# Moving the tail of the group norm into the next pair of heads, in an RWKV-7 recurrence on TensorE

## The reference, cut to what matters

```python
kk = kk / jnp.maximum(jnp.sqrt(jnp.sum(kk * kk, axis=-1, keepdims=True)), 1e-12)   # the key norm
a_vec, b_vec = -kk, kk * a_h
S = S * w_t + (S @ av_t) (x) bv_t + v_t (x) k_t ;  y_t = S @ r_t                    # over the tokens
mu, var = mean(y), mean((y - mu)**2)                                               # over the 64 of a head
yn = (y - mu) * lax.rsqrt(var + GN_EPS) * lnx_w + lnx_b                            # the group norm
out = (yn + bonus) * g ;  bonus = sum(r * k * r_k) * v
```

## Time and profile before

| | |
|---|---|
| median of 3 runs | 2415.04 us (2414.31 to 2415.66) |
| the profiled execution's own time | 2415.23 us |
| its span | 2413.5 us |
| TensorE matmuls busy | 2351.0 us, 97% |
| weight loads busy | 2252.7 us, 93% |
| DVE busy | 1473.5 us, 61% |
| ScalarE busy | 879.6 us, 36% |
| mean granted TensorE clock | 0.996 |

### The profile page before, as it was taken

How to read it: one execution, slowest core, us unless ns; L and a number is a source line. 1 busy time by engine, 2 the same in 40 slices (tenths; PEclk the granted TensorE clock), 3 DMA queues, 4 the chain that set the end, 5 groups by cost and what they waited for, 6 DMA issues and landing times.

```text
span 2413.5 us, 48839 instructions
## 1 busy us (share of the span) xinstructions
PE 2351.0 (97%) x19616; PEld 2252.7 (93%) x19616; DVE 1473.5 (61%) x2125; ACT 879.6 (36%) x1048; POOL 131.3 (5%) x203
## 2 busy tenths in 40 slices
PE   8999999999999999999999998999999999999999
PEld 6899989898888888888999988999999999999998
DVE  5644544566677666776535457665666666566676
ACT  6443344343332233322434344333333333333334
POOL 3000011000000010000001010000000000000003
PEclk9999999999999999999999999999999999999999
DMA  7554487342333243332445633444444444444443
GB/s 267 185 165 142 160 285 251 97 140 90 99 100 96 85 137 96 100 96 86 151 153 160 197 105 105 157 140 143 158 151 149 147 156 140 143 157 151 152 145 110
DMA packets 282189, 346.67 MB, mean 144 GB/s; under 512 B 6957, under 2 KB 240733, under 8 KB 280907
## 3 DMA queue, kind: packets, MB, share of 16 engines
q1 hardware_dynamic: 271883, 307.66, 39.6%
q0 software_dynamic: 9712, 36.30, 4.5%
q10 hardware_dynamic: 464, 0.79, 0.1%
HBM read 333.83 MB, written 10.89 MB: 143 GB/s over the span
## 4 chain that ended last, share of the span: by engine, by line
PE 82%; DVE 10%; issue 4%; ACT 1%; DMA 1%; DVEq 1%; SPq 0%; ACTq 0%
PE bank L246 19%; PE bank L255 19%; PE bank L247 19%; PE bank L227 4%; PE bank L229 4%; PE bank L228 4%; PE bank L1193 3%; DVE work L911 2%; ACT hi L211 1%; DVE lo L218 1%; PE bank L1210 1%; PE bank L511 1%; DVE work L1025 1%; PE bank L512 1%; PE bank L518 1%
## 5 line engine op out<-in xcount | busy, mean ns | idle before, releaser
L218 DVE TENSOR_TENSOR lo<-raw,hi 128x2048 fp32r<-128x2048 f32 x286 | 655.8, 2293 | 502.9 <-ACT hi L211 485.6
L246 PE MATMUL bank<-ah,hi 128*128 128x320 f32 x3200 | 957.4, 313 | 0.2 <-DVE al L532 0.2
L247 PE MATMUL bank<-al,hi 128*128 128x320 f32 x3200 | 945.9, 309 | 0.0
L211 ACT ACTIVATE hi<-raw 128x2048 fp32r<-128x2048 f32 x286 | 548.0, 1916 | 935.1 <-PE bank L255 681.1
L246 PEld LDWEIGHTS bank<-ah,hi 128*128 128x128 f32 x3200 | 601.0, 188 | 15.4 <-issue 13.3
L247 PEld LDWEIGHTS bank<-al,hi 128*128 128x128 f32 x3200 | 601.4, 188 | 0.4
L255 PE MATMUL bank<-ah,lo 128*128 128x320 f32 x3200 | 545.4, 311 | 2.5 <-DVE lo L218 2.5
L255 PEld LDWEIGHTS bank<-ah,lo 128*128 128x128 f32 x3200 | 486.4, 188 | 7.4 <-DVE lo L218 4.1
L227 PE MATMUL bank<-bh,hi 128*128 128x320 f32 x704 | 218.7, 311 | 0.2 <-DVE work L2410 0.2
L229 PE MATMUL bank<-bh,lo 128*128 128x320 f32 x704 | 217.5, 309 | 0.0
L228 PE MATMUL bank<-bl,hi 128*128 128x320 f32 x704 | 217.5, 309 | 0.0
(11 more groups left out here) (386 smaller groups left out, 2090.7 us busy)
## 6 DMA issues: line engine op xcount, KB each, us to landing
raw<-in_w_in SPq DMA_DIRECT2D x98, 1024.0 KB, 5.3
raw<-in_w_up SPq DMA_DIRECT2D x88, 1024.0 KB, 5.1
raw<-in_w_down SPq DMA_DIRECT2D x44, 1024.0 KB, 5.1
raw<-in_w_branch SPq DMA_DIRECT2D x24, 1024.0 KB, 5.5
raw<-in_w_out SPq DMA_DIRECT2D x16, 1024.0 KB, 5.4
raw<-in_w_mem_k SPq DMA_DIRECT2D x8, 1024.0 KB, 5.8
raw<-in_w_mem_v SPq DMA_DIRECT2D x8, 1024.0 KB, 5.2
work<-in_cache_mem_k POOLq DMA_DIRECT2D x8, 1024.0 KB, 6.0
```

The costliest lines, as they stand in the source:

```text
L211: act.activation(hi[c % NS][:, :], raw[c % 2][:, :], ACT.Copy).then_inc(S("hi_done"), 1)
L218: dve.tensor_tensor(lo[c % NS][:, :], raw[c % 2][:, :], hi[c % NS][:, :], ALU.subtract)\
L246: pe.matmul(out, w, xh[:, 8 * h + k, :], start=h + k == 0, stop=False)
L247: pe.matmul(out, w, xl[:, 8 * h + k, :], start=False, stop=False)
```

## The change

The last three operations of the group norm (reciprocal of the root, product, sum) leave the end of a pair and become `norm_out(dve, vv, i)`, run in the next pair behind t_rt and ahead of A2's copy; pair 0 runs it on set values, and one more run stands behind the last pair, at the head of `branch_dve`. The gated rows land one row further on (`row_(1)` to `row_(8)`). What it reads must live across the border of the pairs: `ym` goes to ka_t's place, `ysq` to t_x's; ScalarE puts the bonus into t_ck, without waiting for `gated_out`, and DVE's bonus product moves ahead of BCt's evictions. ScalarE's wait for `gated_out` now stands ahead of the turned v. The root of the variance stands behind ScalarE's wait for tr0, and so behind the `hi` of the sixth unit. `weights_low(5)` comes ahead of the last branch addition, `weights_low(0)` behind B4. The key norm's two operations, and the product `av` (`prepare_av`) that was the end of `prepare_k`, move between Z2 and Z3. y's copy moves ahead of `prepare_rest`. TensorE's order is unchanged but for the value of one wait.

```diff
--- before.py
+++ after.py
@@ -722,7 +722,7 @@
         step_ = wk[:, 3584:3776]
         sam = wk[:, 8 * T:8 * T + 512].rearrange("p (b v) -> p b v", b=NB)
         vtm = wk[:, 8 * T + 512:8 * T + 1024].rearrange("p (b v) -> p b v", b=NB)
-        y_, ym, ysq = t_x, zc[:, 0:T], zc[:, T:2 * T]
+        y_, ym, ysq = t_x, ka_t, t_x
 
         cum, ldx, pt = be, ka, t_bk
         rk = t_bo
@@ -838,7 +838,18 @@
             tmp = t_bd if first else row_(j + 15)
             vv.do(dve.tensor_scalar(tmp, av, -1.0, pcol("k_a", j), ALU.add, ALU.mult))
             vv.do(dve.scalar_tensor_tensor(out=row_(j + 8), in0=tmp, scalar=1.0, in1=row_(j + 8), op0=ALU.add, op1=ALU.mult))
+            if first:
+                prepare_av(dve, vv)
+
+        def prepare_av(dve, vv):
             vv.do(dve.tensor_tensor(av, kkv, av, ALU.mult))
+
+        def norm_out(dve, vv, j):
+
+            dve.wait_ge(S("gn_root"), j + 1)
+            vv.do(dve.reciprocal(ysq, ysq))
+            vv.do(dve.tensor_tensor(ym, ym, ysq, ALU.mult))
+            vv.do(dve.tensor_tensor(row_(j), ym, bon, ALU.add), "gated_out")
 
         def prepare_al(dve, vv, j):
             dve.wait_ge(S("exps"), 3 * (j + 1))
@@ -867,6 +878,9 @@
             vv.do(dve.memset(alm, 0.0))
 
             vv.do(dve.memset(st_[0], 0.0), "ring_out")
+            vv.do(dve.memset(ym, 0.0))
+            vv.do(dve.memset(bon, 0.0))
+            vv.do(dve.memset(ysq, 1.0), "gn_root")
             vv.do(dve.memset(st_[1], 0.0), "gated_out")
             for c in range(2):
                 vv.do(dve.memset(gs[:, c, :], 0.0), "gate_free")
@@ -939,18 +953,18 @@
                     vv.do(dve.tensor_copy(zc3[:, cs[0]:cs[-1] + 1, 0:64], c3(pbank(name)[:, 0:k])))
                     tt(zc3[:, cs[0]:cs[-1] + 1, 64:128], c3(pbank(name)[:, k:2 * k]), m_in[:, cs[0]:cs[-1] + 1, :], ALU.mult, "ring_out")
                 tt(c5(t_rt), c5(t_ad), bmid(m_id[:, :], NC), ALU.add)
+                norm_out(dve, vv, i)
                 plain(t_a2, "A2")
                 plain(t_b2, "B2")
+                dve.wait_ge(S("turned_out"), OUT0_A + N_OUT_A * i + OUT_A["bonus"] + 1)
+                tt(bon, t_ck, row_(i + 16), ALU.mult)
                 for name, cs in (("BCt", TURNED), ("BCs", UPRIGHT)):
                     ps(name)
                     part(t_bk, name, 0, cs, m_st)
                     part(t_ck, name, 64 * len(cs), cs, m_in, "ring_out")
-                weights_low(0)
                 plus(t_rt, "RT1")
                 plain(t_bd, "B4")
-                dve.wait_ge(S("turned_out"), OUT0_A + N_OUT_A * i + OUT_A["bonus"] + 1)
-                tt(bon, bon, row_(i + 16), ALU.mult)
-                prepare_norm(dve, vv, i + 1)
+                weights_low(0)
                 plus(t_rt, "RT2")
                 prepare_k(dve, vv, i + 1)
                 plain(t_a2, "Q", TP)
@@ -966,6 +980,8 @@
                 prepare_logs(dve, vv, i + 1)
                 plain(t_rt, "QT4", TP)
                 plus(zc, "Z2", 512)
+                prepare_norm(dve, vv, i + 1)
+                prepare_av(dve, vv)
                 plus(zc, "Z3", 512)
                 ps("X4")
                 tt(t_x[:, TP:T], t_x[:, TP:T], pbank("X4")[:, 0:64], ALU.add, "ring_out")
@@ -1000,9 +1016,9 @@
                 prepare_al(dve, vv, i + 1)
                 branch(0, 1)
                 prepare_kk(dve, vv, i + 2)
-                prepare_rest(dve, vv, i + 1)
                 dve.wait_ge(S("y_ps"), i + 1)
                 vv.do(dve.tensor_copy(y_, bank[6][:, 0:T]), "y_out")
+                prepare_rest(dve, vv, i + 1)
                 ps("g")
                 vv.do(dve.scalar_tensor_tensor(out=bon, in0=bon, scalar=pcol("lnx_b", i), in1=bank[6][:, 0:T],
                                                op0=ALU.add, op1=ALU.mult))
@@ -1020,12 +1036,8 @@
                 ps("var")
                 vv.do(dve.tensor_scalar(ysq, pbank("var")[:, 0:T], 1.0 / HD, GN_EPS, ALU.mult, ALU.add), "ring_out")
                 prepare_ops(dve, vv, i + 1)
+                weights_low(5)
                 branch(1, 1)
-                dve.wait_ge(S("gn_sqrt"), i + 1)
-                vv.do(dve.reciprocal(ysq, ysq))
-                tt(ym, ym, ysq, ALU.mult)
-                tt(row_(i), ym, bon, ALU.add, "gated_out")
-                weights_low(5)
 
         def bmid(ap, n):
 
@@ -1046,10 +1058,10 @@
             if ps:
                 i = j - 1
                 ps("bonus")
-                act.wait_ge(S("gated_out"), j)
-                aa.do(act.activation(bon, pbank("bonus")[:, 0:T], ACT.Copy), "turned_out")
+                aa.do(act.activation(t_ck, pbank("bonus")[:, 0:T], ACT.Copy), "turned_out")
                 act.wait_ge(S("wkv_ps"), PS0 + NPR * i + PR["ssq"] + 1)
                 aa.do(act.activation(sq, pbank("ssq")[:, 0:T], ACT.Sqrt), "kk_root")
+                act.wait_ge(S("gated_out"), j + 1)
                 for name, c, k in (("vkt", 0, 128), ("vks", 128, 192)):
                     ps(name)
                     o = pbank(name)
@@ -1083,9 +1095,10 @@
             if beside:
                 beside.due(10 ** 6)
             if ps:
-                ps("mean")
+                ps("tr0")
                 act.wait_ge(S("ring_out"), OUT0 + N_OUT * j)
-                aa.do(act.activation(ysq, ysq, ACT.Sqrt), "gn_sqrt")
+                act.activation(ysq, ysq, ACT.Sqrt).then_inc(S("gn_root"), 1)
+                act.wait_ge(S("gn_root"), j + 1)
                 for m in range(2):
                     ps(f"tr{m}")
                     aa.do(act.activation(s_out[:, 512 * m:512 * m + 512], pbank(f"tr{m}")[0:64, :], ACT.Copy), "turned_out")
@@ -1095,7 +1108,7 @@
             aa.do(act.activation(v_, row_(j + 16), ACT.Copy), "v_copied")
 
         def wkv_act(act, aa, n):
-            with aa.loop(4 * n, 4 * n + 4, {"act": 2, "low_out": 2, "exps": 3, "kk_root": 1, "v_copied": 1, "gn_sqrt": 1, "turned_out": N_OUT_A}) as i:
+            with aa.loop(4 * n, 4 * n + 4, {"act": 2, "low_out": 2, "exps": 3, "kk_root": 1, "v_copied": 1, "turned_out": N_OUT_A}) as i:
                 units = [0]
 
                 def stream(p):
@@ -1349,7 +1362,7 @@
 
                 o = begin("S4", "X1")
                 wait("sam_ready", i + 1)
-                wait("gated_out", i + 1)
+                wait("gated_out", i + 2)
                 sam_, vtm_ = [x.rearrange("p b v -> p (b v)") for x in (sam, vtm)]
                 y_terms(0, 0, start=True)
                 heads(o[:, :], [(zb(NCK), sam_)], stop=False)
@@ -1892,8 +1905,8 @@
         def branch_act(act, aa):
 
             tile_ready(act, U_BR[2] - 1)
-            act.wait_ge(S("gated_out"), KW + 1)
-            aa.do(act.activation(bh[:, :, :], rw[:, 0:KW, 0:T], ACT.Copy), "bh_ready")
+            act.wait_ge(S("gated_out"), KW + 2)
+            aa.do(act.activation(bh[:, :, :], rw[:, 1:KW + 1, 0:T], ACT.Copy), "bh_ready")
             with act.Fori(8, 11) as i:
                 for j in range(6):
                     branch_act_unit(act, j, i)
@@ -1914,8 +1927,9 @@
                                            in1=ah[:, 4 * c:4 * c + 4, :], op0=ALU.mult, op1=ALU.subtract), "mx_lo")
 
         def branch_dve(dve, vv):
+            norm_out(dve, vv, KW)
             dve.wait_ge(S("bh_ready"), 2)
-            vv.do(dve.tensor_tensor(bl[:, :, :], rw[:, 0:KW, 0:T], bh[:, :, :], ALU.subtract), "bl_ready")
+            vv.do(dve.tensor_tensor(bl[:, :, :], rw[:, 1:KW + 1, 0:T], bh[:, :, :], ALU.subtract), "bl_ready")
             with vv.loop(8, 11, {"gate_free": 4}) as i:
                 for g in range(2):
                     for h in range(3):
```

## The result

The changed kernel takes 2437.9 us (median of 4 runs, 2435.63 to 2438.69) against 2415.35: ratio 1.0089, 95% interval 1.0072 to 1.0107. It is slower by 22.6 us where I had forecast 5.6 and a range that ended at 2428. The profiled execution took 2435.63 us, with a span of 2433.6 us and a mean granted clock of 0.988, for 0.996 before. It is the fastest of the four; the other three, with a mean clock of 0.986 to 0.987, took 2 to 3 us more.

The account below looks back on a forecast made before the run. TensorE, busy nearly all the span, was taken to bound the kernel. Terms of 3.2 + 1.5 + 1.2 - 4.5 - 0.4 = +1.0 us, plus 4.6 for clock falls, gave 5.6 on 2415.23: 2420.8 us, range 2413.5 to 2428.

Parts of the forecast that it names:

- rival 1: The clock falls in nearly every pair: 12 to 14 us, with 1.0 more, 2428 to 2430 us; chance 0.22.
- the nine: New TensorE idles of 3.4 us, eight in pairs, one behind them; three or four followed by clock falls, +4.6 us.
- The first stall goes: ScalarE's bonus eviction, and the root behind it, no longer wait for the norm's sum; stall 1.4 us at the longest.
- The second grows: A2's copy on DVE stands behind t_rt and the norm, so TensorE idles 3.4 us ahead of BCt in every pair.
- Pair 0 longer by 2.7 us: Sign expected in the profile after: pair 0, which no group norm preceded, gets the new stall and grows by 2.7 us.
- The others alike within 0.2: Sign expected in the profile after: the pairs other than pair 0 are alike within 0.2 us.
- y's copy, -4.5 us: y's copy ahead of prepare_rest starts some 0.7 us sooner and the stall before g goes: -4.5 us over eight pairs.
- Key norm beside Z3 covered: Operations of 3.3 to 3.4 us between Z2 and Z3 fit DVE's 4.05 us wait for TensorE, 0.7 us to spare.
- Behind the last pair an idle of 3.4 us in place of one of 2.5: Ahead of the third unit, the new wait replaces the old and the slow matmuls that followed it: -0.4 us.
- From BCt to the turned v 5.1 us: Without the `lo` ahead of RT1's addition this way takes 5.1 us, between 5.0 and 5.26, in every pair.
- The `lo` moved behind B4, the root behind tr0, the memsets: Three moves or additions on DVE, on ScalarE and at the start, each claimed to cost nothing.
- Sum without the clock +1.0 us: All terms except falls of the granted clock: 3.2 + 1.5 + 1.2 - 4.5 - 0.4 = +1.0 us.

Follow-up runs that it names:

- e8_fill2: The changed kernel with two matmuls of constants, never read, in TensorE's idle ahead of BCt, leaving about 2.5 us of idle: 2423.48 us.
- e7_y_alone: The kernel before with only y's copy moved ahead of prepare_rest: 2411.23 us, ratio 0.9976.
- e1_fill: The changed kernel with five matmuls of constants, never read, issued in TensorE's idle ahead of BCt: 2420.04 us, ratio 1.0014.
- e3_steps: The changed kernel with the three stream steps ahead of RT1 put ahead of BCt: 2407.98 us, ratio 0.9964.
- e4_free: The changed kernel with the norm's operands in free rows, norm_out between Z2 and Z3, key norm back behind B4, weights_low(0) ahead of RT1: 2398.95 us.
- e6_split: e4_free with weights_low(0) and then the key norm behind B4, and the gated rows' rounding behind the last pair cut in two: 2390.06 us.

## Why the prediction was wrong

The sign and the mechanism (A2's copy late, one long idle ahead of BCt, falls of the clock behind it) were right, the size was off by a factor of four, and the time lies 10 us outside the range. What came about was rival 1, to which I had given a chance of 0.22, and the loss was larger than rival 1 allowed. The step that failed is this one: "How many of the nine are answered can't be read from one case: none to nine, 0 to +14 us. [...] I take three or four, +4.6 us." All nine were answered. In the profiled execution the eight in the pairs cost 16.9 us and the ninth 1.5 us, 18.4 us for 4.6.

Three things were in it.

**The number.** Idles of 1.88 us (not answered) and 2.48 us (answered) were in the trace, and the new ones were to be 3.4 us, longer than both. I let "one case only" pull the count to the middle of its range, while the rows that were there pointed one way. And there was more than one case: the prediction's rows stop at the end of the stage, but behind it the same trace of the kernel before has an idle of just the length in question, 3.60 us, and one of 5.57 us, and half clock beside both. Its matmuls behind the two idles, and the stretches:

```profile
1435.17 0.41 PE L477 MATMUL bank<-ident,rw 128*128 128x128 f32 x2 [3.60 <-DVE mix L2070]
1456.10 0.60 PE L2135 MATMUL bank<-ah,hi 128*128 128x320 f32 x1 [5.57 <-DVE al L2075]
```

```profile
1436.70:1440.00 3.30, 3.30 (x10) 2.30 (x10) 3.09 (x7) 1.88 (x4) 2.99 (x5) 0.50 0.00 0
1453.80:1460.50 6.70, 4.40 (x17) 4.43 (x17) 6.35 (x11) 2.95 (x4) 0.00 (x0) 0.50 0.00 1
```

The fall beside the second lasted 6.8 us, a length that my price for one fall left out. The argument that a place in time may escape is true at 2.3 to 2.6 us (seven of eight in e8_fill2, and the very idle of 2.48 us in e7_y_alone) and was false at 3.6 (none of 14 in and behind the pairs). So the answer at 2.48 us was itself one that another execution didn't give; the idle of 3.60 us was what should have moved the count.

**The length of one fall.** I took the 1.5 us that the fall of 3.4 us had cost as the most. Five of eight falls lasted 6.8 us and cost 2.3 to 2.8 us each; rival 1, at 12 to 14 us, was too small for that reason as well.

**The range.** It ended at the near end of rival 1 instead of holding it, and a term that is paid nine times was given the bounds of one.

The Trainium skill, TensorE: Matmul & The Clock Gate, section HAM oscillation, says that each burst of matmuls behind a long wait begins throttled again. That gave the right count here: the trace of the changed kernel agrees nine times of nine. The waits of that section are of 3 to 5 us; of the shorter idles of e8_fill2, 2.30 to 2.59 us, one of eight was answered.

Point by point, the rest stood. *The first stall goes:* gone. *The second grows, as A2's copy is late:* 3.58 to 3.87 us of idle, with 3.4 forecast; of the 0.2 to 0.5 us more, the rows show a gap ahead of the copy of beCs in pairs 0 and 1 (0.47 and 0.24 us), one of 0.52 ahead of A2's copy in pair 4, and one of 0.1 ahead of the reciprocal, none of which pair 0 of the kernel before has. *Pair 0 longer by 2.7 us:* 2.87 without the clock (75.34 in e1_fill against 72.47). *The others alike within 0.2:* 75.11 against 75.10 in pair 1, but 75.35 against 75.69 in pair 4 (e1_fill against the kernel before). *y's copy, -4.5 us:* in e7_y_alone pairs 0 to 6 are shorter by 0.52 to 0.74 us each, 3.95 together, and the eighth would make it 4.5. *Key norm beside Z3 covered:* DVE still waits 0.81 us there. *Behind the last pair an idle of 3.4 us in place of one of 2.5:* 3.60. *From BCt to the turned v 5.1 us:* 5.11 in e1_fill. *The `lo` moved behind B4, the root behind tr0, the memsets:* no wait in which any of them shows. *Sum without the clock +1.0 us:* +1.9 in the stage.

## What to carry to other kernels

An idle of TensorE had two prices here, its length and what the clock did afterwards; in most pairs two stalls of 1.3 us and one of 0.5 became one of 3.6, which left the idle time nearly alike, and cost 17 us by the clock. When a step is moved off one critical place, write down what TensorE waits for next in its own fixed order: here that was a plain copy of 0.5 us, and 3.3 us of DVE work had been put ahead of it. Where a stall can't be removed, put work that is due anyway into it (three steps of the stream, 30 us better), or at the least break it up; and ask first whether only a buffer ties the moved work to its place, as it did here.

## What the runs showed of the hardware that I had not expected

- A fall of the granted clock lasted 3.4 or 6.8 us behind idles of the same length (3.6 us). In the pairs of the changed kernel's profiled execution the five that began 0.4 to 1.7 us ahead of the idle's end lasted 6.8, the three that began later 3.4. A fall of 3.4 us cost 1.4 to 1.5 us, one of 6.8 us 2.3 to 2.8 us.
- The idle of 1.88 us in the attention stage, followed by the full clock in the kernel before, is followed by a fall at 472.6 in the changed kernel, from instructions that the change doesn't touch. Over all ten traces, each of another kernel with these same instructions, seven show the fall and three (the kernel before, e3_steps, e4_free) don't. So an idle's answer can differ between executions, and one trace without a fall is no proof that an idle is safe. In the recurrent stage no idle of up to 1.73 us (e6_split) was answered in any trace. Stretches of the changed kernel, the idle and what follows:

```profile
469.70:471.70 2.00, 0.12 (x2) 0.08 (x2) 1.76 (x7) 0.74 (x1) 0.00 (x0) 1.00 0.71 188
472.70:476.00 3.30, 3.30 (x16) 3.30 (x15) 0.50 (x2) 1.77 (x3) 3.30 (x1) 0.50 0.25 87
```

- Five matmuls of constants in each pair, 2.96 us that did no work, delayed nothing that could be seen (in pair 1 BCt comes 9.33 us behind ABt with them and 9.34 without) and gave back 18 us.
